# A fifth slot for the split weights, its memory taken from the descriptor scratch of the GpSimd queue

## What is computed

```python
def first_block(x, c, ...):
    mod = silu(c) @ ada_w + ada_b                     # 2048 x 12288, one row
    h = modulate(rms_norm(x, norm1_g), sh1, sc1)
    u, lru_gate, q, k, v, mix_gates = split(h @ w_in + b_in)
    y_lru = rg_lru(conv(u)) * gelu(lru_gate)
    y_attn = sliding_window_attention(q, k, v, sinks)
    merged = gate_lru * (y_lru @ w_lru_out) + gate_attn * (y_attn @ w_attn_out)
    x = x + g1 * (merged @ w_o)
    gate, up = split(modulate(rms_norm(x, norm2_g), sh2, sc2) @ w_ffn_in)
    x = x + g2 * ((silu(gate) * up) @ w_ffn_out)
    return rms_norm(x, final_g)

def second_block(x, ...):
    xh, c_q, c_kv, k_pe = split(rmsnorm(x) @ w_in)
    y_hyena = x0 * long_conv(x1 * v)                  # by DFT matrices
    y_attn = mla(c_q, c_kv, k_pe)                     # 8 heads
    h = x + rmsnorm(concat(y_hyena, y_attn) @ w_out)
    g, u = split(rmsnorm(h) @ w_up)                   # 2048 x 11264
    return h + rmsnorm((gelu(conv(g)) * u) @ w_down)
```

## Time and profile before

| | us |
|---|---|
| median of 3 runs | 2740.47 |
| lowest and highest | 2739.61, 2742.82 |
| profiled execution, its span | 2740.2 |
| PE busy | 2689.6 (98%) |
| DVE busy | 1887.5 (69%) |
| ACT busy | 1316.7 (48%) |
| POOL busy | 30.3 (1%) |

### The profile page before, as it was taken

One profiled execution on the slowest core, in us unless ns is written; L12 is line 12 of the kernel. 1 busy time (PEld: TensorE's weight loads), 2 busy tenths in 40 slices (PEclk: granted clock), 3 DMA queues, 4 the chain that ended last, 5 costly groups with the idle time before them and its releaser, 6 DMA issues.

```text
span 2740.2 us, 34009 instructions
## 1 busy us (share of the span) xinstructions
PE 2689.6 (98%) x13316; PEld 2259.4 (82%) x13316; DVE 1887.5 (69%) x2561; ACT 1316.7 (48%) x1874; POOL 30.3 (1%) x60
## 2 busy tenths in 40 slices
PE   8999999999999999999999999999999999999998
PEld 5888888888887788888888888878888888888886
DVE  7878777878876665544554577778577757765775
ACT  4158675544444544344434465544454434543453
POOL 0100000000000000000000000000000000000000
PEclk9999999999999999999999999999999999999999
DMA  9964667799886676555555555443555555555553
GB/s 366 409 247 162 221 200 262 269 348 351 320 277 231 232 270 212 194 190 192 188 196 189 187 187 180 174 139 132 192 168 197 194 194 184 186 199 193 187 193 126
DMA packets 161833, 598.60 MB, mean 218 GB/s; under 512 B 18152, under 2 KB 18377, under 8 KB 160393
## 3 DMA queue, kind: packets, MB, share of 16 engines
q1 hardware_dynamic: 154824, 564.71, 60.4%
q0 software_dynamic: 6848, 31.72, 3.0%
HBM read 592.17 MB, written 4.19 MB: 218 GB/s over the span
## 4 chain that ended last, share of the span: by engine, by line
PE 90%; DVE 5%; DMA 2%; ACT 2%; issue 1%; POOL 0%; SPq 0%; DVEq 0%; ACTq 0%
PE PS L680 89%; DMA W<-in_ada_first 2%; DVE ACC L1958 1%; DVE WL L1955 1%; ACT WH L1312 1%; PE PS L898 0%; DVE G L1955 0%; DVE G L1958 0%; PE PS L1093 0%; DVE XB L1955 0%; DVE TT L1955 0%; DVE G L1961 0%; ACT L1538 0%; PE PS L1035 0%; DVE XBf L1961 0%
## 5 line engine op out<-in xcount | busy, mean ns | idle before, releaser
L1955 DVE TENSOR_TENSOR WL<-W,WH 128x1024 fp32r<-128x1024 f32 x876 | 1065.2, 1223 | 669.0 <-ACT WH L1312 667.7
L1312 ACT ACTIVATE WH<-W 128x1024 fp32r<-128x1024 f32 x876 | 920.1, 1057 | 794.3 <-PE PS L680 722.3
L680 PE MATMUL PS<-XA,WH 128*128 128x512 f32 x2480 | 800.6, 399 | 7.5 <-DVE WL L1955 4.6
L680 PE MATMUL PS<-WH,XA 128*128 128x512 f32 (+1 forms) x2560 | 797.6, 390 | 6.7 <-DVE XA L1955 6.2
L680 PE MATMUL PS<-WH,XB 128*128 128x512 f32 x1952 | 612.0, 391 | 0.7 <-DVE G L1955 0.7
L680 PEld LDWEIGHTS PS<-WH,XA 128*128 128x128 f32 x2560 | 479.6, 188 | 107.3 <-DVE XA L1955 7.8
L680 PEld LDWEIGHTS PS<-XA,WL 128*128 128x128 f32 x2480 | 467.1, 188 | 106.8 <-issue 0.7
L680 PE MATMUL PS<-WL,XA 128*128 128x512 f32 (+1 forms) x1280 | 495.9, 387 | 0.0
L680 PE MATMUL PS<-XA,WL 128*128 128x256 f32 x2480 | 492.4, 278 | 0.0
L680 PEld LDWEIGHTS PS<-WH,XB 128*128 128x128 f32 x1952 | 366.4, 188 | 77.0 <-DVE G L1955 1.0
L680 PEld LDWEIGHTS PS<-XA,WH 128*128 128x128 f32 x2480 | 385.4, 189 | 11.9 <-DVE WL L1955 6.1
(11 more groups left out here) (230 smaller groups left out, 1361.5 us busy)
## 6 DMA issues: line engine op xcount, KB each, us to landing
W<-in_w_ffn_in SPq DMA_DIRECT2D x176, 512.0 KB, 4.1
W<-in_w_up SPq DMA_DIRECT2D x176, 512.0 KB, 4.3
W<-in_w_in SPq DMA_DIRECT2D x132, 512.0 KB, 4.2
W<-in_ada SPq DMA_DIRECT2D x128, 512.0 KB, 5.4
W<-in_w_ffn_out SPq DMA_DIRECT2D x88, 512.0 KB, 3.6
W<-in_w_down SPq DMA_DIRECT2D x88, 512.0 KB, 4.3
W<-in_ada_first SPq DMA_DIRECT2D x64, 512.0 KB, 9.0
W<-in_w_mix SPq DMA_DIRECT2D x64, 512.0 KB, 5.4
```

Source lines behind the costliest of these rows:

```text
L680: return e.matmul(o, l, r, start=start, stop=stop, skip_group_check=True)
L1312: return e.activation(o, a, ACT.Copy)
L1955: return e.tensor_tensor(o, a, b, op)
```

## The change

USLOTS goes from 4 to 5. `WH` and `WL` each get a fifth slot of 4 KB per partition, 8 KB in all, and so `WU` has ten places instead of eight. The program is built with 8192 bytes per partition for the descriptors of GpSimd's DMA queue in place of the default 16384. Nothing else is edited; all that depends on USLOTS follows.

```diff
-USLOTS = 4
+USLOTS = 5
...
-    nc = bacc.Bacc("TRN2", target_bir_lowering=False, num_devices=1)
+    nc = bacc.Bacc("TRN2", target_bir_lowering=False, num_devices=1, dynamic_dma_scratch_size=8192)
```

## The result

| us | before | after |
|---|---|---|
| median | 2741.98 (12 runs) | 2735.23 (12 runs) |
| lowest and highest | 2737.97, 2743.21 | 2733.81, 2739.11 |
| profiled execution, its span | 2740.2 | 2732.0 |

The ratio is 0.9976, with a 95% interval from 0.9968 to 0.9983: 6.6 us less, between 4.7 and 8.8. The forecast was 4.9 us less, 2735.6 us. It was reckoned from 2740.5 us; in this comparison the kernel before has a median of 2741.98.

What follows compares the result with a forecast made beforehand. PE was taken as the bound, busy 2689.6 of 2740.2 us. Terms 1.33 + 0.55 + 0.6 + 1.92 + 0.5 = 4.9 us, from 2740.5 to 2735.6 us; forecast case 2734.5 to 2737 (0.50), whole range 2732.5 to 2740.2.

Steps and rivals of the forecast that it cites:

- The step: At each boundary ACT and DVE make unit u+4, not u+3, so each low half is ready one unit (2.79 us) sooner.
- Restarts, 0.5 us: PE's first products after waits: an estimated 0.1 us lost at each of five stops, 0.5 us regained.
- Stage gt: Two waits of PE for low halves in stage `gt`, 1.12 and 0.21 us, both go: 1.33 us.
- Stage lo: Two waits of PE for low halves in stage `lo`, 0.27 and 0.28 us, go: 0.55 us.
- Start of the group: Last group of four: the 1.35 us wait goes, a new `XA` wait of some 0.7 us comes: 0.6 us gained.
- Behind the group: Behind the last group of four, PE's wait of 1.92 us for a low half goes whole.
- The loads by GpSimd: First stage: three loads start up to 2.8 to 5.2 us earlier; effect 0, between -1.3 and +3.8 us.
- The smaller scratch: Halved descriptor room for GpSimd's loads costs nothing as long as it takes three 512 KB transfers: 0 us.
- The stop moves on: Rival: waits for softmax, a bank or `XA` replace those for `WL`, half given back, 2738 us; chance 0.18.
- DVE's backlog shrinks too: Rival: an ada sum fills DVE's idle time in `gt`; four waits, 3.15 us, could shrink; 2732.5 us; chance 0.20.
- The early loads: Rival: GpSimd's earlier loads get in the way of ada pieces, +3.8 us, 2739.4 us; chance 0.06.
- the scratch: Rival: halved room takes only one transfer, GpSimd's loads come 7.7 us apart, 2827 us; chance 0.06.

Runs made afterwards that it cites:

- the first experiment: The changed kernel with its five slots, but ACT and DVE make units no further ahead than before: 2741.28 us against 2742.90, ratio 0.9995.

## Why the prediction was right, and where its sizes were off

**The step was right.** All six waits for `WL` went, with the fifth slot but the old order they stay (the first experiment), and the total lies in the range. That the median, 2735.23, all but meets the forecast of 2735.6 is luck: the kernel before had 2741.98 in this comparison and not 2740.5. The gain, 6.6 us, is above the 6 us that I had given as the forecast's upper end; from 2740.5 it leads to 2733.9, which I had given to the rival with the backlog. The result is 0.24% less; I had given less than 0.2% the larger chance, and so was wrong in size by 1.7 us, or 1.9 by the traces (6.8 against 4.9).

**The term that was mis-sized: "Restarts, 0.5 us".** I estimated 0.1 us for each of five stops. The rows of the kernel before show what is missing, at the stop of 393.51:

```profile
391.99 0.40 PE L680 MATMUL PS<-XA,WH 128*128 128x512 f32 x1
...
393.84 0.40 PE L680 MATMUL PS<-XA,WL 128*128 128x256 f32 x2
```

Products in this stage begin 0.23 us apart, while each is shown with a duration of 0.40. The one after 391.99 was due at 392.22 and began at 393.51, a delay of 1.29 us, of which the idle time in brackets shows 1.12. The next began 0.33 us later and not 0.23. So the stop cost 1.29 + 0.10 = 1.39 us: its idle time and 0.27 us, of which I had only the 0.10 behind it. Behind the group it is the same: 1.92 us shown, 2.20 us gained.

It also means that a stop shorter than 0.17 us has no idle row at all between such products, and behind the transposes (L1035) even one of 0.36 us has none. In `gt` there were such stops. Before, in the timelines of PE and of its weight loads:

```profile
360.62 0.49 PE L1035 MATMUL PS<-IDN,G 128*128 128x128 f32 x3
361.23 0.50 PE L680 MATMUL PS<-XA,WH 128*128 128x512 f32 x1
```

```profile
361.22 0.19 PEld L680 LDWEIGHTS PS<-XA,WH 128*128 128x128 f32 x1 [0.36 <-DVE WL L1955]
```

After, the product follows 0.25 us behind, not 0.61:

```profile
360.16 0.49 PE L1035 MATMUL PS<-IDN,G 128*128 128x128 f32 x3
360.41 0.47 PE L680 MATMUL PS<-XA,WH 128*128 128x512 f32 x1
```

The view of waits for the weight loads comes closer to the whole, 7.9 us over nine times:

```profile
PEld PS L680 <- DVE WL L1955: 7.9, 9, 2.2
```

After the change the weight loads wait 1.1 us more for the new `XA` (2.9 us over three times, 1.8 over two before). The difference, 6.8 us, is what the traces measured. Stage by stage it fits less well, and part of the agreement is chance: in `gt` these waits are 2.14 us for 2.78 gained, in `lo` 1.80 for 1.36, at the start of the group 1.75 - 1.1 = 0.65 for 0.48, and behind it 2.24 for 2.20.

**Point by point.**

- *Stage gt:* 1.33 forecast, 2.78 gained. The distance from the product at 377.62 to the one at 399.66 fell from 22.04 to 20.18 us (376.80 to 396.98 after): 1.86 us for the two known stops. The other 0.92 us were stops without an idle row, at 357.7 (0.17 us), 361.2 (0.36) and 400.3 (0.38). That no new wait took their place is the sums' doing: without their move the stage gained 1.05 us. The prediction moved the low halves alone in its working and gave the sums, which move too, no price here.
- *Stage lo:* 0.55 forecast, 1.36 gained. The two known stops gave 0.62 us each, 0.35 us more than their idle time each. Two more have no idle row, but the weight loads wait there for `WL`, 0.17 us at 643.09 and 0.24 us at 689.14; they gave 0.05 and 0.09 us. Against the other kernels with the old order the stage gained 2.1 to 2.9 us, so this may be the term that was furthest off. The ring did not use up the stock.
- *Start of the group:* 0.6 forecast, 0.48 gained. The new wait came where and for what was forecast, at 0.90 us and not 0.7: the group could begin at 1978.32, which in the old trace is 1983.82, and not at the forecast 1983.99.
- *Behind the group:* 1.92 forecast, 2.20 gained.
- *The loads by GpSimd:* 0 forecast between -1.3 and +3.8; 0.9999 [0.9990, 1.0008] alone, so between 2.7 us of gain and 2.2 of loss, with no sign of either. None of these loads waits for PE any more, as forecast. The DMA traffic of the stage is unchanged, 410 GB/s after, 409 before.

```profile
60.00:120.00 60.00, 56.99 (x267) 48.69 (x267) 50.20 (x79) 7.26 (x16) 7.40 (x14) 0.97 1.03 410
```

- *The smaller scratch:* 0 forecast, 0.9998 alone. The sign that I had named for too little room, GpSimd standing ahead of an issue, shows at 1024 bytes, at one issue of the last eight, 2.66 us, and in small at 2048 bytes: in both traces with that size it stands for 0.18 us ahead of the load `G<-in_idft` (L661), where it doesn't with 4096 and more. The Trainium skill ("DMA: Bandwidth & Descriptors", "The descriptor swizzle" and "Terms") was the base of an estimate of far more room than is used; nothing at 8192 and 4096 bytes speaks against it. At 1024 bytes it fails: by it there was room for some seven transfers, and GpSimd stood with three under way, as the bytes of the four outputs before them had all been moved by 2720.5 us.

**The rivals.** *The stop moves on* came true at one place only, the one in the sum. *DVE's backlog shrinks too* had one half right: the sum falls into the idle time of `gt`, and that is worth 1.73 us, for which it had no price. Its price came from the four waits from 1990.56 to 2017.04, and these stayed as long as they were, as was said against it:

```profile
1984.58 0.39 PE L680 MATMUL PS<-XA,WH 128*128 128x256 f32 x1 [0.88 <-DVE XA L1958]
...
2011.06 0.50 PE L680 MATMUL PS<-XA,WH 128*128 128x512 f32 x1 [1.28 <-DVE G L1955]
```

*The early loads* and *the scratch* did nothing.

## What to carry to other kernels

A deeper buffer pays only through what the producers then make earlier; the free slot alone gave nothing measurable, and if other work shares a ring with the producers, it must move ahead with them. Price a stop of PE by the distance of its products' starts, or roughly by the wait of its weight loads (7.9 us here), and not by the idle time of its products (5.2 us), since at the stop worked out above the shown end of a pipelined product covered 0.17 us and the restart took another 0.1. And look at what stands behind the last byte: here it was 5.6 us of 2740, and one argument of the program shortened it.

## What the runs showed that I had not expected

- The time from the last byte to the end of the span goes by the scratch of GpSimd's queue: 5.6 us at 8192 and 16384 bytes, 3.2 at 4096, 2.2 at 2048, 1.0 at 1024. Below 16384 two or three kernels were traced at each size, and they agree.
- A scratch of 1024 bytes is enough for 28 loads of 512 KB at 4.35 us apart; it made GpSimd wait once at the end, 2.66 us, with eight outputs of 256 KB close together.
- Holding back the sums of 128 pieces in a ring of six made the changed kernel 27.6 us slower; a seventh place gave back 20 us of it by the medians, 12.6 by the traces.
- A queue's waits can change their name and not their sum: SyncE waited 546 us for sums in place of 282, and 2324 us in all in place of 2316.
- The granted clock fell in one short stretch of a trace, 0.66 over 5 us, and cost some 1.1 us there; in another execution the dip lay elsewhere. With the sums held back the clock was 0.96 over 175 us.
